# Front of a hybrid diffusion step: tokens fetched first, norm by chunk, eight modulation buffers, no hardware loops, router logits in four column groups

## The reference

```
sh1, sc1, g1, sh2, sc2, g2 = split(silu(cond) @ w_ada + b_ada, 6)   # w_ada is 1024 x 6144
h = rms_norm(x, norm1_g) * (1 + sc1) + sh1
u = h @ w_in            # GLU input | q, k, v | branch gates
conv = pointwise(silu(layer_norm(depthwise31(val * sigmoid(gate)))))
attn = neighbourhood or context attention(q, k, v)
x = x + g1 * ((sigmoid(g_a) * conv + sigmoid(g_b) * attn) @ w_out)
h = rms_norm(x, norm2_g) * (1 + sc2) + sh2
aff = softmax(h @ w_router)                  # w_router is 1024 x 16
each of 16 experts takes its top 128 latent and top 32 context tokens: SwiGLU, weighted, added back
x = x + g2 * moe;  y = rms_norm(x, final_g)
```

## Time and profile before

| | |
|---|---|
| median of 3 runs | 2895.55 us (2894.99 to 2898.88) |
| profiled execution | 2895.31 us, of which the profile's span is 2893.5 us |
| busy: PE, DVE, ACT, POOL | 2706.2, 1710.9, 1247.9, 189.9 us |
| transfers | 543.50 MB, mean 188 GB/s |

### The profile page before, as it was taken

The page is one execution under the profiler, slowest core; times in us unless marked ns, Lnnn a source line. Parts: engine busy times, 40 slices in busy tenths (PEclk is TensorE's granted clock), DMA queues, the critical chain, the costliest instruction groups (busy, mean ns, idle before and its releaser), DMA issues.

```text
span 2893.5 us, 49953 instructions
## 1 busy us (share of the span) xinstructions
PE 2706.2 (94%) x21599; PEld 2015.0 (70%) x21599; DVE 1710.9 (59%) x2017; ACT 1247.9 (43%) x1772; POOL 189.9 (7%) x175
## 2 busy tenths in 40 slices
PE   5999998999899999958999999999999999999994
PEld 3555585666566697726777777777777777777773
DVE  4008886676322234465666767676767676766664
ACT  2000115555212122224565656565556555555554
POOL 0000001110000000000101110111011100110000
PEclk9999998999999999978999999999999999999997
DMA  7222112000333354164878888898788888888884
GB/s 250 84 76 86 59 47 55 14 1 2 92 92 90 92 151 159 73 225 164 276 268 280 283 277 270 276 290 270 275 277 290 270 274 277 290 270 273 275 278 162
DMA packets 457488, 543.50 MB, mean 188 GB/s; under 512 B 26304, under 2 KB 409387, under 8 KB 457290
## 3 DMA queue, kind: packets, MB, share of 16 engines
q1 hardware_dynamic: 449610, 519.60, 55.2%
q0 software_dynamic: 7680, 20.98, 3.2%
HBM read 513.27 MB, written 27.28 MB: 187 GB/s over the span
## 4 chain that ended last, share of the span: by engine, by line
PE 86%; DVE 8%; ACT 3%; DMA 1%; issue 1%; SPq 1%; DVEq 0%; POOL 0%; ACTq 0%; POOLq 0%
PE bank L624 81%; PE bank L627 5%; DVE slot_lo L1757 3%; ACT e_hi L1315 1%; ACT arena L1176 1%; DVE arena L1804 1%; DVE arena L1529 1%; ACT arena L1174 1%; DVE arena L1695 0%; DVE arena L1694 0%; DMA arena<-in_w_ada 0%; DVE arena L1825 0%; DVE arena L1697 0%; DVE arena L1539 0%; SPq L381 0%
## 5 line engine op out<-in xcount | busy, mean ns | idle before, releaser
L624 PE MATMUL bank<-arena 128*64 128x128 f32 (+8 forms) x3696 | 756.5, 417 | 64.6 <-ACT arena L1176 14.1
L1757 DVE TENSOR_TENSOR slot_lo<-slot,e_hi 128x2048 fp32r<-128x2048 f32 x256 | 579.2, 2288 | 187.9 <-ACT e_hi L1315 184.5
L624 PEld LDWEIGHTS bank<-arena 128*128 128x128 f32 (+4 forms) x3696 | 434.4, 167 | 347.5 <-issue 243.8
L1315 ACT ACTIVATE e_hi<-slot 128x2048 fp32r<-128x2048 f32 x256 | 481.4, 1917 | 1.9 <-DMA xhat<-arena 1.9
L624 PE MATMUL bank<-e_hi,xe_hi 128*128 128x512 f32 x1024 | 418.1, 408 | 0.0
L624 PE MATMUL bank<-e_hi,xe_lo 128*128 128x512 f32 x1024 | 404.7, 395 | 0.0
L624 PE MATMUL bank<-slot_lo,xe_hi 128*128 128x512 f32 x1024 | 400.2, 391 | 0.0
L624 PE MATMUL bank<-slot,arena 128*32 128x128 f32 (+1 forms) x10240 | 366.4, 297 | 24.9 <-DVE arena L1767 22.4
L624 PEld LDWEIGHTS bank<-slot,arena 128*32 128x32 f32 x10240 | 284.6, 110 | 94.8 <-issue 56.4
L1761 DVE TENSOR_TENSOR slot_lo<-slot,e_hi 128x2048 fp32r<-128x2048 f32 x128 | 288.8, 2287 | 77.9 <-ACT e_hi L1317 77.9
L627 PE MATMUL bank<-arena 128*128 128x128 f32 (+4 forms) x1423 | 207.4, 280 | 55.7 <-DVE arena L1703 25.5
(11 more groups left out here) (185 smaller groups left out, 2533.7 us busy)
## 6 DMA issues: line engine op xcount, KB each, us to landing
slot<-in_w_gate_e SPq DMA_DIRECT2D x128, 1024.0 KB, 5.8
slot<-in_w_up_e SPq DMA_DIRECT2D x128, 1024.0 KB, 9.2
slot<-in_w_down_e SPq DMA_DIRECT2D x128, 1024.0 KB, 6.9
arena<-in_w_in SPq DMA_DIRECT2D x68, 512.0 KB, 5.1
arena<-in_w_ada SPq DMA_DIRECT2D x48, 512.0 KB, 4.7
arena<-in_w_conv_pw SPq DMA_DIRECT2D x24, 256.0 KB, 5.5
arena<-in_w_attn_o SPq DMA_DIRECT2D x24, 256.0 KB, 5.3
yacc<-arena SPq DMA_DIRECT2D x10, 512.0 KB, 2.6
```

Source lines behind the costliest of these rows:

```text
L624: return nc.tensor.matmul(out, lhsT, rhs, start=start, stop=stop)
L1315: A_(halves(e_hi[c % 2])[:, :, rows4, :], halves(slot[q])[:, :, rows4, :], ACT.Copy).then_inc(ehi_ok, 1)
L1757: V_.tensor_tensor(halves(slot_lo[q])[:, :, rows4, :], halves(slot[q])[:, :, rows4, :], halves(e_hi[c % 2])[:, :, rows4, :].bitcast(F32), ...
```

## The change

It has four parts. **Front:** the three chunks of tokens are fetched ahead of the tiles of `w_ada`, and tiles 0 to 7 get eight buffers, so that SP waits for no tile. The squares are shared out by row tile between DVE (even) and ACT (odd), root, reciprocal and scaling are done per chunk, and PE turns chunk 0 before tile 0, chunk 1 before tile 2 and chunk 2 before tile 4. **Loops:** every `Fori` becomes a Python loop, so that its body stands in the program once for each turn. **Router:** `wr` is padded with zeros to 32 columns for each k, the eight products go to the four column groups, so that four partial sums lie on the partitions 0, 32, 64 and 96, ACT copies all 128 partitions to `lgT`, and the ten transposes become ten products with `sel`, a 128 x 16 matrix that adds the four parts. **Small:** GpSimd clears `wr`, DVE makes `sel`, `w_router` is fetched after the pads are cleared.

```diff
         ws = [at(R + 2048 * i, KD, 256) for i in range(4)]
+        ws += [at(o, KD, 256) for o in (CONV, CONV + 2048, Q, Q + 2048)]
...
-        wr = const(KD, NE)
+        wr, sel = const(KD, 32), const(NE)
...
-            for s in range(4):
+            for s in range(3):
+                x_rows = A["x_sample"][0, 512 * s:512 * s + 512] if s < 2 else A["x_prompt"][0]
+                sp.dma_start(xin[:, 4 * s:min(4 * s + 4, NT), :], x_rows.rearrange("(t p) d -> p t d", p=P)).then_inc(x_in[s], 16)
+            for s in range(8):
                 ada_load(s, 256 * s)
-                if s < 3:
-                    x_rows = A["x_sample"][0, 512 * s:512 * s + 512] if s < 2 else A["x_prompt"][0]
-                    sp.dma_start(xin[:, 4 * s:min(4 * s + 4, NT), :], x_rows.rearrange("(t p) d -> p t d", p=P)).then_inc(x_in[s], 16)
-            for s in range(4):
-                sp.wait_ge(ada_ready, s + 1)
-                ada_load(s, 1024 + 256 * s)
-            sp.dma_start(wr, A["w_router"][0].rearrange("(k p) n -> p k n", p=P)).then_inc(wr_in, 16)
+            sp.wait_ge(pads, 1)
+            sp.dma_start(wr[:, :, 0:NE], A["w_router"][0].rearrange("(k p) n -> p k n", p=P)).then_inc(wr_in, 16)
...
             for s in range(8):
-                pe.wait_ge(ws_in[s % 4], 32 * (s // 4) + 32)
+                if s in (0, 2, 4):
+                    turn(xin, s // 2, xs1, t1_ready, t1_act, t1_dve, 0)
+                pe.wait_ge(ws_in[s], 32)
                 pe.wait_ge(ada_copied, s + 1)
-                ada(s % 4, 6 + s % 2)
+                ada(s, 6 + s % 2)
                 ada_turn(6 + s % 2, s + 1)
-                if 4 <= s < 7:
-                    turn(xin, s - 4, xs1, t1_ready, t1_act, t1_dve, 0)
...
-                with pe.Fori(0, 2) as i:
+                for i in range(0, 2):
...
-                    last = mm(bank[tc][0:NE, 0:n], wr[:, k, :], h2T[:, k, t0:t0 + n], k == 0, k == KD - 1)
+                    g = 32 * (k % 4)
+                    last = mm(bank[tc][g:g + 32, 0:n], wr[:, k, :], h2T[:, k, t0:t0 + n], k < 4, k >= 4)
...
-                last = tr(bank[3][:, NE * t:NE * t + NE], lgT[:, P * t:P * t + P], NE)
+                last = mm(bank[3][:, NE * t:NE * t + NE], lgT[:, P * t:P * t + P], sel, True, True)
...
+            row_squares(1)
+            row_squares(3)
+            row_deviation(0)
+            row_squares(5)
+            row_squares(7)
+            row_deviation(1)
+            turned(0)
+            ada_tile(0)
+            row_squares(9)
+            row_deviation(2)
+            ada_tile(1)
+            turned(1)
+            ada_tile(2)
+            ada_tile(3)
+            turned(2)
+            for s in range(4, 8):
+                ada_tile(s)
...
+            row_squares(0)
+            row_squares(2)
+            scale_rows(0)
+            row_squares(4)
+            row_squares(6)
+            turned(0)
+            scale_rows(1)
+            row_squares(8)
+            scale_rows(2)
+            turned(1)
+            turned(2)
```

More of the change, by code:

```diff
@@ L256, in backbone @@
         wo_in = [sem(f"wo_in{q}") for q in range(KD // 2)]
-        ws_in = [sem(f"ws_in{i}") for i in range(4)]
+        ws_in = [sem(f"ws_in{i}") for i in range(4)] + wo_in
         wm_in = [sem(f"wm_in{i}") for i in range(2)]
@@ L408, in _ @@
                     n = 8 + 2 * j + a
-                    sp.wait_ge(ada_ready, n - 1)
+                    sp.wait_ge(ada_ready, n - 1 if j else 3 + a)
                     ada_load(2 + a, 256 * n)
@@ L455, in _ @@
             for tc in range(3):
-                with sp.Fori(0, 3) as i:
+                for i in range(0, 3):
                     for s in range(2):
@@ L842, in _ @@
             for tc, (t0, n) in enumerate(TOK):
-                with pe.Fori(0, 4) as i:
+                for i in range(0, 4):
                     for s in range(2):
@@ L1064, in _, with row_squares, row_deviation, turned @@
             act.wait_ge(u_free, 3)
-            for s in range(8):
+            def row_squares(t):
+                act.wait_ge(x_in[t // 4], 16)
+                if t > 1:
+                    act.wait_ge(sq1_act, t // 2)
+                A_(arena[:, R + 9216:R + 9216 + D], xin[:, t, :], ACT.Square, accum_out=ss[:, t:t + 1]).then_inc(sq1_act, 1)
+            def row_deviation(tc):
+                t0, t1 = 4 * tc, min(4 * tc + 4, NT)
+                act.wait_ge(sq1, t1 // 2)
+                act.wait_ge(sq1_act, t1 // 2)
+                A_(std[:, t0:t1], ss[:, t0:t1], ACT.Sqrt, bias=eps, scale=1.0 / D).then_inc(std1, 1)
+            def turned(tc_):
+                for g, (c, tc) in enumerate(tile_groups()):
+                    if g % 2 == 0 and tc == tc_:
+                        t0, n = TOK[tc]
+                        act.wait_ge(t1_ready, g + 1)
+                        A_(hT[:, c, t0:t0 + n], bank[g % 4][:, 0:n], ACT.Copy).then_inc(t1_act, 1)
+            def ada_tile(s):
                 ada_row_copy(6 + s % 2, s + 1)
@@ L1103, in _ @@
                        scale=A1[:, c, cnd:cnd + 1]).then_inc(h_act, 1)
-            with act.Fori(0, 2) as i:
+            for i in range(0, 2):
                 for jj in range(2):
@@ L1225, in _ @@
             for tc, (t0, n) in enumerate(TOK):
-                with act.Fori(0, 3) as i:
+                for i in range(0, 3):
                     for s in range(2):
@@ L1269, in logits_copy @@
                 act.wait_ge(lgT_ready, tc + 1)
-                A_(lgT[:, t0:t0 + n], bank[tc][0:NE, 0:n], ACT.Copy).then_inc(lgT_ok, 1)
+                A_(lgT[:, t0:t0 + n], bank[tc][:, 0:n], ACT.Copy).then_inc(lgT_ok, 1)
             norms(0)
@@ L1404, in _ @@
             dve.wait_ge(idents, 5)
+            V_.tensor_reduce(sel, ident.rearrange("p (g c) -> p c g", c=32)[:, 0:NE, :], AX_X, ALU.add)
             V_.tensor_reduce(csum, ident.rearrange("p (g c) -> p c g", c=32)[:, 0:2, :], AX_X, ALU.add).then_inc(cs_ok, 1)
@@ L1410, in _, with row_squares @@
             dve.wait_ge(colv_ok, 1)
-            for t in range(NT):
-                if t % 4 == 0:
-                    dve.wait_ge(x_in[t // 4], 16)
+            def row_squares(t):
+                dve.wait_ge(x_in[t // 4], 16)
                 if t:
-                    dve.wait_ge(sq1, t)
+                    dve.wait_ge(sq1, t // 2)
                 V_.tensor_tensor_reduce(arena[:, R + 8192:R + 8192 + D], xin[:, t, :], xin[:, t, :], 1.0, 0.0,
@@ L1462, in _ @@
             dve.wait_ge(pads, 1)
-            with dve.Fori(0, 2) as i:
+            for i in range(0, 2):
                 for jj in range(2):
@@ L1472, in _ @@
             base = steps[0]
-            with dve.Fori(0, KC) as k:
+            for k in range(0, KC):
                 def row(t, off, w):
@@ L1593, in _ @@
             for tc, (t0, n) in enumerate(TOK):
-                with dve.Fori(0, 3) as i:
+                for i in range(0, 3):
                     for s in range(2):
```

35 lines of the change are left out of this document (13 added, 22 removed).

## The result

The changed kernel takes 2880.75 us (median of 5 runs, 2879.34 to 2881.79) beside 2895.55 us for the kernel before in the same session (5 runs, 2894.12 to 2898.88): 14.8 us less, ratio 0.9948 with a 95% interval of 0.9933 to 0.9962. The forecast was 2878.0, its range 2868 to 2887. The profiled execution took 2880.47 us, its span is 2878.7 us.

The account below looks back on a forecast made before the run. PE, with 86% of the chain of waits, was taken to bound the kernel. Front 6.2, loops 0.4 and router 10.8 sum to 17.4 us off the profiled 2895.31, giving 2877.9 (2878.1 against the median), range 2868 to 2887.

Parts of the forecast that it names:

- The first turning at 21.5: Front: chunk 0 lands at 14.4 us, squares end at 16.9, and root, reciprocal and scalings let PE start turning at 21.5.
- The turning done at 27.4: Front: chunk 0's turning takes 5.14 us plus about 0.8 us of PE standing for DVE's and ACT's delayed copies.
- Tiles 0 and 1 at the slow pace, 34.3: Front: the two tiles after the first turning take 3.46 us each, PE at half speed, ending at 34.3 us.
- costs nothing: Front: ACT's wait for DVE's tile 8 delays tile 1's copies to near 32.4 us, when PE has about finished tile 1's products.
- Turning 1 at 4.1: Front: chunk 1's turning, 3.69 to 5.14 us before, is taken as 4.1 us, ending at 38.4.
- Tiles 2 to 7 at the fast pace, u at 56.7: Front: these tiles run fast, 4.1 us for two and 8.3 for four; u starts at 56.7, not 62.89, saving 6.2 us.
- The rival of the low clock for tiles 4 to 7: Front: these tiles stay slow, costing 5.7 us, giving 2883.8; chance 0.22, shared with a router whose clock stays low.
- The u phase at half rate: Start of the u phase: half rate for 6 us after the idle 3.84, costing 3.1 us, assumed to stay.
- The loops, 0.4 us saved: All loops written out: only the 0.43 us gap entering the u phase's second half closes, saving 0.4 us, bounds 0 and 1.
- the rival of the straight code: PE's 30 added bodies each wait for instructions; from 0.58 us each the gain is gone, at 1 us 2908; chance 0.03.
- The router, 10.8 us saved: Router: grouped products save 12.4 us, the ten products with `sel` lose 1.6, so 10.8 us saved.
- The bound for a half-rate router: Router: if PE were at half rate throughout, products of 3.9, 3.9 and 1.9 and 4.5 us would give back 6.4 us.

Follow-up runs that it names:

- e4: The changed kernel once more, unaltered: 2881.15 us, 12.9 us less than the kernel before.
- e12: e11 plus one unread filler product in each front tile (four at tile 1) and eight ahead of the first output tile: 2874.08 us.
- e2: The kernel before with the front part alone, hardware loops and router as before: 2888.23 us, 5.8 us less than the kernel before.
- e7: The changed kernel with eight unread filler products on PE ahead of the u phase's first half: 2874.02 us.
- e9: The changed kernel with SP's merge loop alone put back as a hardware loop: 2881.97 us.
- e10: The changed kernel with PE's merge loop alone put back as a hardware loop: 2876.75 us.
- e8: The changed kernel with the old order of transfers, a tile of w_ada ahead of each chunk of tokens: 2882.52 us.
- e6: The changed kernel with ACT copying tile 1 and chunk 1's turned groups before chunk 2's root, and DVE copying chunk 1 before squaring tile 8: 2880.49 us.
- e3: The kernel before with its nine hardware loops written out, nothing else: 2896.65 us, 2.6 us more than the kernel before.
- e5: The changed kernel with every hardware loop put back, so front and router parts only: 2877.49 us.
- e11: e5 with the eight filler products of e7 ahead of the u phase's first half: 2877.28 us.

## Why the prediction was right, and where its terms were off

The forecast of 2878.0 was 2.75 us (0.1%) too low, well within its range. The mechanism held: a shift of the front, carried to the end, and a shorter router. That the total came so near is in part luck, for terms that were off by 1 to 2 us each way cancel. Step by step, by the prediction's own numbers:

**The first turning at 21.5.** Right: 21.44. Chunk 0's squares began at 14.24 (14.4 foreseen), and the root, reciprocal and four scalings came as costed.

**The turning done at 27.4.** 28.03, but for another reason. It took 6.59 us, for 5.14 and the 0.8 of the new wait. PE has no such wait: its products come 0.213 us apart without a gap up to 27.43, and 0.109 us apart from there. The whole excess is half pace, which the prediction had put at nothing here beyond what the 5.14 us contained. In the second profile of the same kernel (e4) the pace changes at 24.64, 3.4 us behind the turning's start instead of 6.0, and the turning took 5.31.

**Tiles 0 and 1 at the slow pace, 34.3.** Wrong in both halves, near in the sum. They ran at the fast pace (1.07 us for `ada`, not 1.94). But the sentence that ACT's wait "costs nothing" failed: it held up tile 1's small products by 2.28 us instead of the usual 0.51. I had found the wait and its place, 32.4 for the end of the copies (33.4 in fact), and had laid it against a PE at the slow pace; at the fast pace PE was there 1.8 us before. The next turning began at 33.89. (The "faster end" of these two tiles, 2.5 us less in the prediction, is 2.8 by its own two paces.)

**Turning 1 at 4.1.** 5.36, since the clock fell at 34. That is a price of the wait that the prediction didn't have: not the 1.8 us alone, but also about 1.7 us of the turning (5.36 for 3.69). The filled variant (e12) shows both ends: without the idle stretch the turning takes 3.69. The changed kernel's profile is among the mild ones: in e2, e4, e7, e9 and e10, with the same wait, this turning took 6.2 to 6.5 us.

**Tiles 2 to 7 at the fast pace, u at 56.7.** Right in kind, 2.11 us apart for the 2.04 to 2.08 that I had used, and the way from the last tile to the u phase as before, 4.00 for 3.84 idle: 57.81. So the front gave 5.1 at that point, not 6.2. The rival of the low clock for tiles 4 to 7 was not far: the clock fell at the last of these tiles in e2, e4, e8, e9 and e10, at a cost of about 1 us each, and for more of them in e6. The prediction had let a warm stretch without a long idle piece stay warm; these profiles don't bear that out.

**The u phase at half rate.** "The same idle stays, so I leave it in": half right. The grant fell already during the idle time and was back sooner, and the first half took 151.9 us for 153.1. These 1.2 us I hadn't counted; with 0.6 for the gap between the halves and a little in the attention the lead was 7.2 at the third chunk of the merge, for 6.6 foreseen.

**The loops, 0.4 us saved.** The term itself was about right (0.6), and the sign of the part as a whole probably wrong: e3 gives +2.6 us with an interval that reaches to no change, and e10, with one loop put back, is 5.2 us under e9. I had looked for stalls at the heads of PE's bodies, as the rival of the straight code has it, and the trace has none. The cost sits on another engine: late weights in the merge (1.2 us in this profile), which by e9 and e10 hang on TensorE's straight code. The rest was lost in the gate rows, where the link with the straight code is only a correlation. In e3's profile the two places cost 0.7 and 1.6 us. The Trainium skill, page "Runtime: NRT & Kernel Launch", section "Instruction fetch mechanics", gives the fetch at a taken branch as a reason to unroll; the runs show one gap of that kind, 0.4 us on the chain, and against it +2.6 us for the loops' part alone (interval -0.6 to +4.6 us).

**The gate rows.** Not in the prediction at all. PE begins them at 1094.16 and they take until the first output projection at 1106.69, 12.53 us for 10.79 before. The grant there was 0.50 from 1096 on; before it was 1.00 up to 1110. A lead of 1.7 us went there. It fell so early in three of the seven profiles with PE's merge written out (after, e3, e6) and in none of the seven with the loop. That is a correlation, and its cause stays open: e9 had the latest weights of all and kept its clock.

**The router, 10.8 us saved.** 11.1 in the whole kernel, and -11.3 for the kernel with that part alone. The products took 2.97 and 2.79 us (3.0 and 2.95 foreseen), the last twenty passes 2.40 (2.4 foreseen). The bound for a half-rate router, 6.4 in the prediction, is about 5.9 by its own terms (3.75 in the products, 2.1 in the last ten). Between grouped products and whole-array turnings the rows at 1239.88 and 1242.18 show no gap. The Trainium skill, page "TensorEngine Tiling (Array Packing)", section "Tiling Modes", has a drain at such a switch; no row here shows one.

**The sum.** Foreseen 6.2 + 0.4 + 10.8 = 17.4. Measured: 7.2 up to the merge, -1.2 in its last chunk, -1.7 in the gate rows, -0.1 up to the router, +11.1, and -0.4 from there to the end: 14.9, by the spans 14.8. What is short in the total are mostly two losses outside the two places of the change: the late weights, a side effect of the third part, which I had costed at PE alone, and the gate rows, whose cause is open. The front's own 1.1 us too little were made good by the shorter half-rate spell behind it. Between two profiles of the same kernel (after and e4) the lead at the first output projection differs by 2.0 us, so the split holds to about that; the two medians of the same kernel, against the kernel before, differ by 1.9 us.

## What to carry to other kernels

Where a wait on the bottleneck engine seems to cost only its length, add what the granted clock does behind it, and look whether a few products whose results nobody reads, put where the engine would stand, buy more than they cost: here eight of them saved 1.7 to 1.9 us at their place (and 5 to 7 us in one kernel, for reasons not all known), and 19 more, 11 of them in the front, brought 3.2. Writing the loops out was worth here the gap that the trace shows at their turns and no more; its cost can appear on another engine's transfers, so look at the weights' arrival, not only at the heads of the bodies. Cost a wait at both paces of the engine that it is laid against.

## What the runs showed of the hardware that I had not expected

The granted clock fell not only in long idle stretches. In e2, e4, e8, e9 and e10 it fell in the middle of tiles that were 2.11 us apart, with PE idle 0.51 us ahead of the small products of each, and the same rows ran at full rate in the changed kernel's profile and in e5, e7 and e11. With the idle time filled (e12) the grant stayed at 1.00. A single profile doesn't tell the pace of such a stretch.

The first turning went at half pace for its first part although the windows read 1.00 there. In the changed kernel, with PE busy all the time, the window from 22 to 24 us has 11 of these products, and from 24 to 26 us 12; from 34 to 36 us, where 0.56 is granted, it has 13; in e6 at 32 to 34 us, granted 1.00 and at full pace, there are 20. The trace's list of clock entries settles it. In the changed kernel the first entry begins at 27.41 us, and the first product of the turning at the fast pace begins at 27.43; in the kernel before it is 45.10 and 45.14, in e4 24.60 and 24.64. In thirteen of the fourteen traces the two times lie within 0.07 us of each other, and in e8 the entry (33.06) lies within a tile's `ada`, whose products come closer from there. Ahead of the first entry there is no record of the clock, and a window without a record reads 1.00. So the slow tiles at 33.77 in the kernel before, which the prediction met "though the granted clock reads 1.00", ran at the lower level by their pace, and the kernel came out of it in the middle of the first turning. At full pace this turning takes 3.69 us; in the kernel before its first 3.0 us went at the lower level and it took 5.14, in the changed kernel the first 6.0 us, and it took 6.59.

Column groups gave what they promise: eight products of 512 columns took 8.07 us in one group of 16 columns and 2.97 in four, each with about 2.1 us at the lower clock, and the 768 columns that follow took 10.49 and 2.79, both at full rate.
